# The last three gathered rows fetched in halves, and two weight chunks rounded on GpSimd

## The chip, the cores and the metric

The kernel runs on one core of one Trainium2 chip. The metric is the device time of one execution in microseconds, the median over several runs. The program is written by hand: every engine (TensorE, ScalarE, VectorE, GpSimd, and SyncE for transfers) has its own list of instructions, and semaphores tie them together.

## What is computed

Two transformer blocks follow each other on 256 tokens of width 1024. The change lies at the seam between them, so this is the part that must be seen:

```python
def block(args):                      # end of the first block: a mixture of 16384 experts
    hb, eb, gb = args
    ub = jnp.take(u, eb, axis=0)      # 8 heads x 16 experts chosen for every token
    z = jnp.einsum('thkd,td->thk', ub, hb)
    a = (jax.nn.gelu(z.astype(jnp.float32)) * gb).astype(hb.dtype)
    return jnp.einsum('thk,thkd->td', a, jnp.take(v, eb, axis=0))
...
x = x + g2[:, None, :] * rms_norm(y, norm2_post[l])      # y is the experts' sum
...
h = rms_norm_2(x, norm1_g[l])                            # the second block begins
proj = h @ w_in                                          # q, k, v, xl, gl
```

## The kernel before, in words

**Experts.** The 256 tokens are two blocks of 128 (a = 0, 1), one token to a partition. An expert's u and v rows lie side by side in one table of 2048 columns, `peer_uv`. A "row" i (0 to 255) below is one gather: for 128 tokens the i-th expert's u and v, 128 x 2048 in f32, 1 MB, 8 KB to a partition. GpSimd issues the 256 gathers in order (L2325), each as soon as its place is free (`ROW_BEFORE`: the place's row before has been combined) and its indices are there. For each row VectorE forms the dot product of the u half with the token (`dot`, L1976), ScalarE the gelu (L1318 for four rows, `last_gelu` L1332 for each of the last eight), VectorE the weight (L1987, L1994), ScalarE a diagonal matrix of it (`diagonal`, L1326), and TensorE adds diagonal times v half to two PSUM banks (L834, two matmuls, which the trace shows as four instructions). `landed(i)` is the semaphore of row i's gather; only `dot` waits for it, since everything else comes behind the dot. The last 32 rows all belong to block a = 1.

**The seam.** After row 255 ScalarE loads the table with the square root (`load_sqrt`, L1058), squares the two banks (`experts_square`, L1071), and VectorE applies the gain, the norm and the residual (`experts_norm`, L1544, L1548), and then the gain of the second block's first norm (L1544 again). TensorE transposes the two halves of the result (`feature_half`, L467), ScalarE rounds each to `hfh` (`features_hi`, L1076) and VectorE makes the rest `hfl` (`features_lo`, L1557). TensorE bridges the time with 34 products that nobody reads (L862). Block a = 0 went through the same seam long before.

**Products.** Each f32 product is made of three in a rounded format: data are split in a high part (ScalarE rounds the weights, `hi`, L1046) and a low part (VectorE subtracts, `lo`, L1514). The weights come in loads of 1 MB, each of two chunks of 128 x 1024. `WQ0 + 16` and `WQ0 + 17` are the first two chunks of q of the second block ("q2"). `token_product("q2", ...)` runs `part` for four chunks: `highs(0)` and `highs(1)` for the token blocks 0 and 1 (L501, L502), then `lows(0)`, `lows(1)` (L507). `highs(1)` of a chunk needs the features of block a = 1, `highs(0)` does not.

**Loads.** SyncE issues the weight loads (L2386). Those of the second block (I_Q2 and after) go to places that rows used: it waits for `landed(254)` and then for the combination of the last row of each place (the fifth one's is row 254). GpSimd, after its gathers, clears `wbd` once the block's features are done (L2333).

Of the kernel before, what the change touches and what calls it, by code (L numbers as in the profile page):

```python
# [10 lines left out]
AF = mybir.ActivationFunctionType  # L11
# [119 lines left out]
def build_program(nc, A, out):  # L131
# [3 lines left out]
    def sem(name):  # L135
        return ctx.enter_context(nc.semaphore(name))
# [6 lines left out]
    chunk_at = {}  # L143
    for n, (name, i, c, kind) in enumerate(chunks):
# [30 lines left out]

    s_adc = sem("s_last_adc")
    s_maxo, s_maxb = sem("s_max_out"), sem("s_max_bcast")
    s_pool, s_flp, s_id, s_const, s_wbd, s_iu = [sem("s_" + n) for n in (
        "pool", "mix_lo", "ident", "consts", "wbd0", "iu")]

# [52 lines left out]
    def landed(i):  # L233
        return s_gath[ROW_SLOT[i]], 16 * ROW_SLOT[:i + 1].count(ROW_SLOT[i])
# [175 lines left out]
    def wo_done(c):  # L410

        return s_chunk, WO0 + WO_B.index(c) + 1

    def split(n):

        assert n < WQ0 or n >= WQ0 + 16
        return n + 1 if n < WQ0 else n - 15
# [38 lines left out]
    def tensor_program(e):  # L456
# [11 lines left out]
            r.then_inc(*o.inc(s_tr, TR[mark]))  # L468

        def split_done(n):  # L470
            e.wait_ge(s_hi, split(n))
            e.wait_ge(s_lov, split(n))
            return chunk_of(n)[2:]

        def high_done(n):
            e.wait_ge(s_hi, split(n))
            return chunk_of(n)[2:]

        def product(name, f, b, xh, xl_, by_k=None):
# [10 lines left out]
                r = e.matmul(pb[:, 0:256], lo[:, k, :], xh[:, k, :], start=False, stop=k == 7)  # L490
            r.then_inc(*o.inc(s_chunk, n + 1))

        def part(n, k0, two, xh, xl_, start, stop, by_k=None, first=None, between=None):
            hi, lo = high_done(n)

            def highs(a):
                for k in range(k0, k0 + 2):
                    if by_k:
                        by_k(k, a)
                    s_ = slice(128 * a, 128 * a + 128)  # L500
                    e.matmul(two[a][:, :], xh[:, k, s_], hi[:, k - k0, :], start=start and k == k0, stop=False)  # L501
                    e.matmul(two[a][:, :], xl_[:, k, s_], hi[:, k - k0, :], start=False, stop=False)  # L502

            def lows(a):
                e.wait_ge(s_lov, split(n))
                for k in range(k0, k0 + 2):
                    r = e.matmul(two[a][:, :], xh[:, k, 128 * a:128 * a + 128], lo[:, k - k0, :], start=False,  # L507
                                 stop=stop and k > k0)
                return r

            highs(0)
            if first:
                lows(0).then_inc(*o.inc(s_first, first))
                if between:
                    between()
                highs(1)
            else:
                highs(1)
                lows(0)
            lows(1).then_inc(*o.inc(s_chunk, n + 1))  # L520

        def token_product(name, b0, b1, xh, xl_, by_k=None, first=None):
            two = [bank(b0), bank(b1)]
            for i in range(4):
                part(chunk_at[name, i], 2 * i, two, xh, xl_, i == 0, i == 3, by_k, first if i == 3 else None)
# [303 lines left out]
        for n, (a, h) in enumerate(ITS):  # L829
            for k in range(16):  # L830
                i = 16 * n + k
                e.wait_ge(s_dg, i + 1)
                for j in range(2):
                    r = e.matmul(acc[a][j][:, :], dg[:, i % 4, :], expert_rows(i)[:, 1024 + 512 * j:1536 + 512 * j],  # L834
                                 start=h == 0 and k == 0, stop=h == 7 and k == 15)
                    if i == 255 and j == 0:
                        r.then_inc(*o.inc(s_first, FIRST["y2", 0]))
                r.then_inc(*o.inc(s_comb, i + 1))
                if i == 0:
                    pb = bank(2)  # L840
                    e.wait_ge(s_q, Q_DONE[0, 1])
                    half_scores(0, 1, pb, 0).then_inc(*o.inc(s_score, SC_DONE[0, 1]))
                    frees[2] = ((s_sct, SC_DONE[0, 1]),)
                for g in QUERY_AT.get(i, ()):
                    query(g)
                if i in SCORE_AT:
                    scores(SCORE_AT[i])
                if i == 235:
                    block_features(0, (0, 1))
# [8 lines left out]

        h3_ready(7, 0)
        pb = bank(0)  # L860
        for _ in range(34):
            e.matmul(pb[:, 0:256], hfh[:, 0, 0:128], hfh[:, 0:2, 0:128], start=True, stop=True)  # L862
        for g in range(2):
            pb = bank(2 + g)
            e.wait_ge(s_hu, 6 + g + 1)
            feature_half(h2t[:, 1, :], pb, g, "h3", 2 + g)
            frees[2 + g] = ((s_flv, FLV["h3", 2 + g]),)
        token_product("q2", 0, 1, hfh, hfl, h3_ready)
        frees[0], frees[1] = ((s_qkt, 1),), ((s_qkt, 2),)
        pb = bank(4)  # L870
        e.wait_ge(s_rd, 4)
# [156 lines left out]
    def scalar_program(e):  # L1028
        o = Own(s_act)

        def hi(n):
            i, v, h, _ = chunk_of(n)
            e.wait_ge(*arrived(i))
            if n == WO0 + 1:
                e.wait_ge(s_flp, FLP["ym", 7])
            elif n == WO0 + 4:
                e.wait_ge(s_mix, 8)
                e.wait_ge(s_fhi, FHI["mix", 7])
                e.wait_ge(s_flp, FLP["mix", 7])
            elif WO0 + 3 <= n < WQ0:  # L1040
                e.wait_ge(s_chunk, WO0)
            elif WQ0 + 16 <= n < WQ0 + 19:
                e.wait_ge(s_chunk, WQ0 + 16)
            elif n >= NB and not WO0 <= n < WQ0:
                e.wait_ge(s_chunk, n - NB + 1)
            e.activation(h, v, AF.Copy).then_inc(*o.inc(s_hi, split(n)))  # L1046

        def taken(name, f):

# [338 lines left out]
            diagonal(i)  # L1388
        load_sqrt()
        experts_square(1)  # L1390
        hi(WQ0 + 16)
        block_square(1)
        hi(WQ0 + 17)
        for g in range(2):
            features_hi(1, g, banks[2 + g], "h3")
        hi(WQ0 + 18)
# [111 lines left out]
    def vector_program(e):  # L1508
        o = Own(s_vec)

        def lo(n):
            _, v, h, l = chunk_of(n)
            e.wait_ge(s_hi, split(n))
            e.tensor_tensor(l, v, h.bitcast(f32), ALU.subtract).then_inc(*o.inc(s_lov, split(n)))  # L1514

        def taken(name, f):
# [454 lines left out]
        def dot(i):  # L1971
            n, row = i // 16, expert_rows(i)[:, 0:1024]
            if i % 16 == 0:
                e.wait_ge(s_wgt, 4 * n - 4) if n >= 2 else e.wait_ge(s_h2s, 2 * n + 2)
            e.wait_ge(*landed(i))
            e.tensor_tensor_reduce(row, row, h2t[:, ITS[n][0], :], 1.0, 0.0, ALU.mult, ALU.add,  # L1976
                                   za[:, n % 2, i % 16:i % 16 + 1]).then_inc(*o.inc(s_dot, i + 1))

# [279 lines left out]
    def gpsimd_program(e):  # L2258
# [46 lines left out]
            e.dma_start(nb[:, :], A[nm][0].partition_broadcast(128)).then_inc(s_nb, 16)  # L2305


        for i in range(256):
            n = i // 16
            e.wait_ge(s_ei8, 1) if i < 8 else e.wait_ge(s_ei, n + 1)  # L2310
            if ROW_BEFORE[i] is not None:
                e.wait_ge(s_comb, ROW_BEFORE[i] + 1)
            elif ROW_SLOT[i] in SLOT_HEAD:
                e.wait_ge(s_chunk, WQ0 + 2 * SLOT_HEAD[ROW_SLOT[i]] + 2)
            elif ROW_SLOT[i] in (4, 5):
                e.wait_ge(s_lov, split(WO0 + (5, 7)[ROW_SLOT[i] - 4]))
            elif ROW_SLOT[i] == 6:
                e.wait_ge(s_tr, TR["sk", 3])
            elif ROW_SLOT[i] == 14:
                e.wait_ge(*wo_done(7))  # L2320
            else:
                e.wait_ge(s_chunk, WQ0)
            a, h = ITS[n]
            at = 16 * h + i % 16
            e.indirect_dma_start(  # L2325
                out=expert_rows(i), out_offset=None, in_=A["peer_uv"],
                in_offset=bass.IndirectOffsetOnAxis(ap=ei[:, a, at:at + 1], axis=0)).then_inc(s_gath[ROW_SLOT[i]], 16)


        e.wait_ge(s_comb, 256)  # L2330
# [11 lines left out]
    def sync_program(e):  # L2342
# [23 lines left out]
        for i in range(8, len(loads)):  # L2366
            if i == I_Q2:
                e.wait_ge(*wo_done(4))
                e.dma_start(g3[:, :], A["norm1_g_2"][0].partition_broadcast(128)).then_inc(s_n2, 16)
            if i == I_Q2 + 5:  # L2370
                e.wait_ge(s_sct, SC_DONE[6, 1])
                e.dma_start(bcs[:, 1, :], A["norm2_g_2"][0].partition_broadcast(128)).then_inc(s_n2, 16)
            if BEFORE[i] is not None:
                released(BEFORE[i])
            elif I_WQ + 6 <= i < I_Q2:
                e.wait_ge(*wo_done(i - I_WQ - 1))
            else:

                e.wait_ge(s_mix, 8)
                e.wait_ge(s_adab, 8)  # L2380
            if I_Q2 <= i < I_Q2 + 5:

                e.wait_ge(*landed(254))
                place = (12, 13, 4, 5, 6)[i - I_Q2]
                e.wait_ge(s_comb, max(r for r in range(256) if ROW_SLOT[r] == place) + 1)
            e.dma_start(places[SLOT[i]], A["weights"][i]).then_inc(s_ring[SLOT[i]], 16)  # L2386
# [34 lines left out]
```

## Time and profile before

| | |
|---|---|
| median of 3 runs | 1277.23 us (1276.95 to 1277.82) |
| the profiled execution | 1276.76 us, its span 1275.0 us |
| TensorE matmuls busy | 1144.0 us (90%) |
| VectorE / ScalarE busy | 909.6 us (71%) / 497.9 us (39%) |
| GpSimd busy | 337.0 us (26%) |
| granted TensorE clock, mean | 0.969 |
| HBM read | 404.66 MB, 318 GB/s over the span |
| chain of work that ended last | PE 43%, DMA 30%, DVE 14%, ACT 7%, issue 5% |

In the tables of the trace PE is TensorE's matmuls, PEld its weight loads, DVE VectorE, ACT ScalarE, POOL GpSimd, SPq SyncE's issue of transfers. L834 is a line of the kernel. "x4" is a number of merged instructions, and the brackets give the idle time of the engine before the row and what ended it. `in_peer_uv` gathers run on the DMA queue q0 (software), weight loads on q1 (hardware); both use the same 16 DMA engines. The experts' part runs from about 326 to 971 us.

### The profile page before, as it was taken

The page shows a single profiled execution, that of the slowest core. Times are in us where ns is not written, and L with a number is a line of the kernel's source. Part 1 is how long each engine was busy: PE and PEld are TensorE (multiplying, and loading weights), DVE is VectorE, ACT ScalarE, POOL GpSimd, SP SyncE. Part 2 cuts the span into 40 slices and gives each one's busy share as a digit, 9 for nine tenths or more (in the row PEclk, how much of TensorE's full clock was granted, in tenths as well). Part 3 has the DMA queues.
Part 4 walks back from the last instruction along what each step waited for, and adds up shares of the span by engine and source line. Part 5 has one row for each costly group of instructions (what it writes and reads, how often), then busy time and mean ns, then how long its engine had stood idle before and what let it go on. Part 6 is the DMA issues. An engine that isn't in the chain of part 4 may idle for free.

```text
span 1275.0 us, 15358 instructions
## 1 busy us (share of the span) xinstructions
PE 1144.0 (90%) x5436; PEld 811.5 (64%) x5436; DVE 909.6 (71%) x1849; ACT 497.9 (39%) x962; POOL 337.0 (26%) x311
## 2 busy tenths in 40 slices
PE   5998999999799999987788878777889999999998
PEld 4978999999655554443333433323336887999787
DVE  5985887786779767777677766677756786666544
ACT  3656454445523222222222222221524477555432
POOL 4000000000356544555554445454451000000000
PEclk8999999999899999999999988899999999999999
DMA  9874387677899999999999999999997523355550
GB/s 357 324 300 163 134 314 266 230 314 296 337 420 419 427 426 426 425 427 427 426 426 427 426 427 427 426 427 425 428 422 303 181 99 130 136 181 184 198 198 33
DMA packets 58272, 406.72 MB, mean 319 GB/s; under 512 B 6964, under 2 KB 7172, under 8 KB 9684
## 3 DMA queue, kind: packets, MB, share of 16 engines
q0 software_dynamic: 38752, 273.55, 51.3%
q1 hardware_dynamic: 19444, 132.19, 27.7%
q8 instruction: 44, 0.72, 0.2%
q14 instruction: 32, 0.26, 0.1%
HBM read 404.66 MB, written 1.06 MB: 318 GB/s over the span
## 4 chain that ended last, share of the span: by engine, by line
PE 43%; DMA 30%; DVE 14%; ACT 7%; issue 5%; POOL 1%; SPq 0%; DVEq 0%; POOLq 0%; ACTq 0%
DMA gbuf<-in_peer_uv,ei 19%; PE bank L834 11%; DMA ring<-in_peer_uv,ei 9%; PE bank L486 5%; PE bank L490 5%; PE bank L487 5%; DVE half L1514 4%; ACT half L1046 4%; PE bank L766 3%; PE bank L1020 2%; PE bank L1021 2%; PE bank L1022 2%; DMA ya<-in_weights 1%; DVE gbuf L1976 1%; PE bank L507 1%
## 5 line engine op out<-in xcount | busy, mean ns | idle before, releaser
L834 PE MATMUL bank<-gbuf,dg 128*128 128x512 f32 x540 | 260.0, 626 | 51.9 <-ACT dg L1326 51.8
L1514 DVE TENSOR_TENSOR half<-ring,half 128x1024 fp32r<-128x1024 f32 x175 | 212.7, 1222 | 123.8 <-ACT half L1046 123.5
L834 PEld LDWEIGHTS bank<-gbuf,dg 128*128 128x128 f32 x540 | 105.2, 199 | 194.2 <-issue 121.7
L1976 DVE CUSTOM_DVE_ANT_0 gbuf<-gbuf,h2t 128x1024 f32<-128x1024 f32 x135 | 165.4, 1226 | 80.8 <-DMA gbuf<-in_peer_uv,ei 78.6
L1046 ACT ACTIVATE half<-ring 128x1024 fp32r<-128x1024 f32 x175 | 182.9, 1052 | 102.2 <-PE bank L1022 45.6
L2325 POOL DMA_INDIRECT gbuf<-in_peer_uv,ei x135 | 166.1, 1230 | 182.7 <-PE bank L834 118.1
L834 PE MATMUL bank<-ring,dg 128*128 128x512 f32 x356 | 173.9, 626 | 31.6 <-ACT dg L1326 30.5
L1318 ACT ACTIVATE za<-za 128x4 f32<-128x4 f32 x62 | 12.7, 205 | 398.4 <-DVE za L1976 398.3
L2325 POOL DMA_INDIRECT ring<-in_peer_uv,ei x89 | 108.1, 1214 | 174.0 <-DVE ei L1949 76.4
L834 PEld LDWEIGHTS bank<-ring,dg 128*128 128x128 f32 x356 | 70.3, 201 | 123.6 <-issue 83.2
L1976 DVE CUSTOM_DVE_ANT_0 ring<-ring,h2t 128x1024 f32<-128x1024 f32 x89 | 108.8, 1225 | 55.6 <-DMA ring<-in_peer_uv,ei 55.1
L486 PE MATMUL bank<-hh,half 128*128 128x256 f32 x448 | 112.8, 289 | 0.9 <-DVE hl L1672 0.7
L487 PE MATMUL bank<-hl,half 128*128 128x256 f32 x448 | 110.2, 283 | 0.0
L1326 ACT ACTIVATE dg<-ident,za 128x128 f32<-128x128 f32 x256 | 82.9, 391 | 37.7 <-DVE za L1987 31.5
L486 PEld LDWEIGHTS bank<-hh,half 128*128 128x128 f32 x448 | 86.1, 192 | 1.9 <-ACT hh L1098 0.8
L487 PEld LDWEIGHTS bank<-hl,half 128*128 128x128 f32 x448 | 86.2, 192 | 0.5 <-issue 0.5
L486 PE MATMUL bank<-hfh,half 128*128 128x256 f32 x304 | 76.5, 290 | 0.0
L487 PE MATMUL bank<-hfl,half 128*128 128x256 f32 x304 | 74.4, 283 | 0.0
L490 PE MATMUL bank<-hh,half 128*128 128x256 f32 x448 | 62.8, 283 | 0.0
L486 PEld LDWEIGHTS bank<-hfh,half 128*128 128x128 f32 x304 | 58.0, 191 | 1.1
L487 PEld LDWEIGHTS bank<-hfl,half 128*128 128x128 f32 x304 | 58.1, 191 | 0.1
L490 PEld LDWEIGHTS bank<-hh,half 128*128 128x128 f32 x448 | 57.8, 192 | 0.0
(434 smaller groups left out, 1916.4 us busy)
## 6 DMA issues: line engine op xcount, KB each, us to landing
ring<-in_weights SPq DMA_DIRECT2D x114, 1024.0 KB, 5.0
gbuf<-in_weights SPq DMA_DIRECT2D x4, 1024.0 KB, 11.2
gbuf<-in_peer_uv,ei POOLq DMA_INDIRECT x135, 22.5
wq_place<-in_weights SPq DMA_DIRECT2D x2, 1024.0 KB, 6.9
bcs<-in_b_ada POOLq DMA_DIRECT2D x3, 512.0 KB, 10.9
ring<-in_peer_uv,ei POOLq DMA_INDIRECT x89
xs<-in_x SPq DMA_DIRECT2D x2, 512.0 KB, 4.3
ya<-in_weights SPq DMA_DIRECT2D x1, 1024.0 KB, 17.0
```

Source lines behind the costliest of these rows:

```text
L486: e.matmul(pb[:, 0:256], hi[:, k, :], xh[:, k, :], start=k == 0, stop=False)
L487: e.matmul(pb[:, 0:256], hi[:, k, :], xl_[:, k, :], start=False, stop=False)
L490: r = e.matmul(pb[:, 0:256], lo[:, k, :], xh[:, k, :], start=False, stop=k == 7)
L766: r = e.matmul(pb[:, s_], v[:, k, :], hf[:, k, s_], start=k == 0, stop=k == 7)
L834: r = e.matmul(acc[a][j][:, :], dg[:, i % 4, :], expert_rows(i)[:, 1024 + 512 * j:1536 + 512 * j], start=h == 0 and k == 0, stop=h == 7 an ...
L1020: e.matmul(q, l_h, hi[:, 0, s_], start=g == 0, stop=False)
L1021: e.matmul(q, l_h, lo[:, 0, s_], start=False, stop=False)
L1046: e.activation(h, v, AF.Copy).then_inc(*o.inc(s_hi, split(n)))
L1326: e.activation(dg[:, i % 4, :], ident[:, :], AF.Copy, scale=za[:, i // 16 % 2, 16 + i % 16:17 + i % 16]).then_inc(*o.inc(s_dg, i + 1))
L1514: e.tensor_tensor(l, v, h.bitcast(f32), ALU.subtract).then_inc(*o.inc(s_lov, split(n)))
L1976: e.tensor_tensor_reduce(row, row, h2t[:, ITS[n][0], :], 1.0, 0.0, ALU.mult, ALU.add, za[:, n % 2, i % 16:i % 16 + 1]).then_inc(*o.inc(s_d ...
L2325: e.indirect_dma_start(out=expert_rows(i), out_offset=None, in_=A["peer_uv"], in_offset=bass.IndirectOffsetOnAxis(ap=ei[:, a, at:at + 1], ...
```

## The change

The last three rows (253, 254, 255) are gathered as six transfers of 128 x 1024: the three u halves, then the three v halves. `dot` waits for its u half (new semaphores `s_last_u`), and TensorE waits for the v half ahead of the combination. SyncE's loads of the second block wait for the u half of row 255 instead of the whole row 254. GpSimd then rounds chunks WQ0 + 16 and WQ0 + 17 (`tensor_copy`, with a semaphore `s_q2hi` of their own), which ScalarE no longer does. TensorE runs 18 instead of 34 products that nobody reads, then `highs(0)` of both chunks (`part_highs`), and only then the two transposes.

```diff
+    def highs_of(n):
+        return (s_q2hi, n - WQ0 - 15) if WQ0 + 16 <= n < WQ0 + 18 else (s_hi, split(n) if n < WQ0 else split(n) - 2)
...
                 e.wait_ge(s_dg, i + 1)
+                if i >= 253:
+                    e.wait_ge(*landed(i))
...
         h3_ready(7, 0)
         pb = bank(0)
-        for _ in range(34):
+        for _ in range(18):
             e.matmul(pb[:, 0:256], hfh[:, 0, 0:128], hfh[:, 0:2, 0:128], start=True, stop=True)
+        two = [pb, bank(1)]
+        for i in range(2):
+            part_highs(chunk_at["q2", i], 2 * i, two, 0, hfh, hfl, i == 0)
         for g in range(2):
...
-        token_product("q2", 0, 1, hfh, hfl, h3_ready)
+        for i in range(4):
+            part(chunk_at["q2", i], 2 * i, two, hfh, hfl, i == 0, i == 3, h3_ready, done=i < 2)
...
         experts_square(1)
-        hi(WQ0 + 16)
         block_square(1)
-        hi(WQ0 + 17)
...
-            e.wait_ge(*landed(i))
+            e.wait_ge(*landed(i)) if i < 253 else e.wait_ge(s_last_u[i - 253], 16)
...
-        for i in range(256):
+        for i in range(253):
...
+        for part in range(2):
+            for i in range(253, 256):
+                a, h = ITS[15]
+                at = 16 * h + i % 16
+                if part == 0:
+                    e.wait_ge(s_comb, ROW_BEFORE[i] + 1)
+                e.indirect_dma_start(
+                    out=expert_rows(i)[:, 1024 * part:1024 * part + 1024], out_offset=None, in_=A["peer_uv"],
+                    in_offset=bass.IndirectOffsetOnAxis(ap=ei[:, a, at:at + 1], axis=0),
+                    element_offset=1024 * part).then_inc(s_gath[ROW_SLOT[i]] if part else s_last_u[i - 253], 16)
+        for c in range(2):
+            i, v, h, _ = chunk_of(WQ0 + 16 + c)
+            e.wait_ge(*arrived(i))
+            e.wait_ge(s_chunk, WQ0 + 16)
+            e.wait_ge(s_comb, 224)
+            e.tensor_copy(h, v).then_inc(*o.inc(s_q2hi, c + 1))
...
-                e.wait_ge(*landed(254))
+                e.wait_ge(s_last_u[2], 16)
```

TensorE at the seam, before (dg is the diagonal, gbuf and ring the rows' places, half_4 and half_0 the rounded chunks of q2, hfh the rounded features):

```order
L834 MATMUL bank<-gbuf,dg 128x512 [waits s_dg]
L834 MATMUL bank<-gbuf,dg 128x512
L834 MATMUL bank<-ring,dg 128x512 [waits s_dg]
L834 MATMUL bank<-ring,dg 128x512
L834 MATMUL bank<-gbuf,dg 128x512 [waits s_dg]
L834 MATMUL bank<-gbuf,dg 128x512
L862 MATMUL bank<-hfh 128x256 [waits s_feat_lo,s_feat_hi]
L862 MATMUL bank<-hfh 128x256 x33
L467 MATMUL bank<-ident,h2t 128x128 [waits s_h_gained,s_q]
```

and now:

```order
L847 MATMUL bank<-gbuf,dg 128x512 [waits s_gather3,s_dg]
L847 MATMUL bank<-gbuf,dg 128x512
L847 MATMUL bank<-ring,dg 128x512 [waits s_gather6,s_dg]
L847 MATMUL bank<-ring,dg 128x512
L847 MATMUL bank<-gbuf,dg 128x512 [waits s_gather7,s_dg]
L847 MATMUL bank<-gbuf,dg 128x512
L875 MATMUL bank<-hfh 128x256 [waits s_feat_lo,s_feat_hi]
L875 MATMUL bank<-hfh 128x256 x17
L505 MATMUL bank<-half_4,hfh 128x512 [waits s_q2_high,s_feat_lo]
...
L505 MATMUL bank<-half_0,hfh 128x512 [waits s_q2_high]
...
L473 MATMUL bank<-ident,h2t 128x128 [waits s_h_gained,s_q]
```

The last three rows have a wait for their gather, and eight products of q2 stand ahead of the transposes in place of 16 unread ones.

GpSimd and SyncE at the end of the gathers, now (before, GpSimd had three gathers of 128x2048 in place of the six and went from them to `wbd`, and SyncE's five loads waited for s_gather6, row 254):

```order
L2349 DMA gbuf<-in_peer_uv,ei 128x1024 [waits s_combine]
L2349 DMA ring<-in_peer_uv,ei 128x1024 [waits s_combine]
L2349 DMA gbuf<-in_peer_uv,ei 128x1024 [waits s_combine]
L2349 DMA gbuf<-in_peer_uv,ei 128x1024
L2349 DMA ring<-in_peer_uv,ei 128x1024
L2349 DMA gbuf<-in_peer_uv,ei 128x1024
L2358 CAST half_4<-ring 128x1024 [waits s_combine,s_chunk,s_ring4]
L2358 CAST half_0<-ring 128x1024 [waits s_combine,s_chunk,s_ring4]
L2364 MEMSET wbd 128x1024 [waits s_feat_hi,s_feat_lo,s_combine]
...
L2417 DMA ring<-in_weights 128x2048 [waits s_combine,s_last_u2] x2
```

The gathers' order is u 253, 254, 255, then v 253, 254, 255, and the two roundings stand behind them.

## Rows read from the trace of the kernel before

**Rows 1.** VectorE, order of time, dots of rows 252 to 255: start, length, what, idle before

```profile
960.04 1.23 DVE L1976 CUSTOM_DVE_ANT_0 gbuf<-gbuf,h2t 128x1024 f32<-128x1024 f32 x1 [0.72 <-DMA gbuf<-in_peer_uv,ei]
...
962.48 1.22 DVE L1976 CUSTOM_DVE_ANT_0 gbuf<-gbuf,h2t 128x1024 f32<-128x1024 f32 x1 [0.71 <-DMA gbuf<-in_peer_uv,ei]
...
964.98 1.23 DVE L1976 CUSTOM_DVE_ANT_0 ring<-ring,h2t 128x1024 f32<-128x1024 f32 x1 [0.77 <-DMA ring<-in_peer_uv,ei]
...
967.40 1.23 DVE L1976 CUSTOM_DVE_ANT_0 gbuf<-gbuf,h2t 128x1024 f32<-128x1024 f32 x1 [0.70 <-DMA gbuf<-in_peer_uv,ei]
```

**Rows 2.** TensorE, order of time, 955 to 989 us

```profile
955.26 12.18 PE L834 MATMUL bank<-gbuf,dg 128*128 128x512 f32 x28
967.27 1.90 PE L834 MATMUL bank<-ring,dg 128*128 128x512 f32 x4
969.61 1.98 PE L834 MATMUL bank<-gbuf,dg 128*128 128x512 f32 x4 [0.44 <-ACT dg L1326]
971.03 4.62 PE L862 MATMUL bank<-hfh 128*128 128x256 f32 x34
975.75 1.29 PE L467 MATMUL bank<-ident,h2t 128*128 128x128 f32 x8
...
977.35 0.39 PE L501 MATMUL bank<-half,hfh 128*128 128x512 f32 x1
977.58 0.40 PE L502 MATMUL bank<-half,hfl 128*128 128x512 f32 x1
978.37 0.47 PE L501 MATMUL bank<-half,hfh 128*128 128x512 f32 x1 [0.40 <-DVE hfl L1557]
```

**Rows 3.** ScalarE, order of time, after the last diagonal

```profile
969.64 1.28 ACT L1058 ACT_TABLE_LOAD   x1
...
971.04 0.58 ACT L1071 ACTIVATE pk<-bank 128x512 f32<-128x512 f32 x1
...
971.63 0.60 ACT L1071 ACTIVATE pk<-bank 128x512 f32<-128x512 f32 x1
...
975.91 1.04 ACT L1046 ACTIVATE half<-ring 128x1024 fp32r<-128x1024 f32 x1
976.85 1.06 ACT L1076 ACTIVATE hfh<-bank 128x512 fp32r<-128x512 f32 x2
```

**Rows 4.** VectorE, order of time, the norms and the features

```profile
971.74 0.69 DVE L1544 TENSOR_TENSOR h2t<-bank,bcs 128x512 f32<-128x512 f32 x1 [2.62 <-ACT pk L1071]
...
977.53 0.69 DVE L1557 TENSOR_TENSOR hfl<-bank,hfh 128x512 fp32r<-128x512 f32 x1 [0.99 <-ACT hfh L1076]
...
980.07 3.49 DVE L1514 TENSOR_TENSOR half<-ring,half 128x1024 fp32r<-128x1024 f32 x3
```

**Rows 5.** DMA packets by queue (number, MB, share of 16 engines), 962.2 to 965 us

```profile
q0 software_dynamic: 10, 0.07, 6.2%
```

**Rows 6.** The same, 965.5 to 966 and 966.5 to 967 us

```profile
q1 hardware_dynamic: 7, 0.06, 95.2%
q0 software_dynamic: 2, 0.02, 7.7%
...
q1 hardware_dynamic: 12, 0.10, 53.6%
q0 software_dynamic: 1, 0.01, 3.9%
```

**Rows 7.** The same, 45.5 to 46 us, loads beside a broadcast of 4 KB rows

```profile
q1 hardware_dynamic: 15, 0.12, 58.7%
q0 software_dynamic: 16, 0.07, 32.8%
```

**Rows 8.** SyncE's issues at the seam (five loads)

```profile
964.97 4.62 SPq L2386 DMA_DIRECT2D ring<-in_weights  x5
```

**Rows 9.** GpSimd, order of time: gathers of rows 253 to 255, and `wbd`

```profile
946.47 0.94 POOL L2325 DMA_INDIRECT gbuf<-in_peer_uv,ei  x1 [0.30 <-issue]
948.18 1.64 POOL L2325 DMA_INDIRECT ring<-in_peer_uv,ei  x1 [0.77 <-PE bank L834]
952.76 1.96 POOL L2325 DMA_INDIRECT gbuf<-in_peer_uv,ei  x1 [2.94 <-PE bank L834]
980.07 0.98 POOL L2333 MEMSET wbd<- 128x1024 f32 x1 [25.35 <-DVE hfl L1557]
```

**Rows 10.** Stretches: us, busy of PE, PEld, DVE, ACT, POOL; then granted clock, DMA, GB/s

```profile
887.54:890.95 3.41, 0.47 (x2) 0.00 (x0) 2.88 (x9) 0.20 (x1) 1.99 (x2) 1.00 1.02 432
890.95:894.36 3.41, 2.96 (x4) 1.40 (x5) 2.41 (x5) 3.36 (x8) 0.00 (x0) 0.50 1.01 428
945.56:948.98 3.42, 1.85 (x5) 0.54 (x3) 2.22 (x4) 0.00 (x0) 2.34 (x3) 1.00 1.01 402
```

More of the change, by code:

```diff
@@ L177, in build_program @@
     s_maxo, s_maxb = sem("s_max_out"), sem("s_max_bcast")
+    s_last_u = [sem(f"s_last_u{i}") for i in range(3)]
+    s_q2hi = sem("s_q2_high")
     s_pool, s_flp, s_id, s_const, s_wbd, s_iu = [sem("s_" + n) for n in (
@@ L470, in split_done @@
         def split_done(n):
-            e.wait_ge(s_hi, split(n))
+            e.wait_ge(*highs_of(n))
             e.wait_ge(s_lov, split(n))
@@ L475, in high_done @@
         def high_done(n):
-            e.wait_ge(s_hi, split(n))
+            e.wait_ge(*highs_of(n))
             return chunk_of(n)[2:]
@@ L491, in product, with part_highs, part @@
             r.then_inc(*o.inc(s_chunk, n + 1))
-        def part(n, k0, two, xh, xl_, start, stop, by_k=None, first=None, between=None):
+        def part_highs(n, k0, two, a, xh, xl_, start, by_k=None):
+            hi = high_done(n)[0]
+            for k in range(k0, k0 + 2):
+                if by_k:
+                    by_k(k, a)
+                s_ = slice(128 * a, 128 * a + 128)
+                e.matmul(two[a][:, :], xh[:, k, s_], hi[:, k - k0, :], start=start and k == k0, stop=False)
+                e.matmul(two[a][:, :], xl_[:, k, s_], hi[:, k - k0, :], start=False, stop=False)
+        def part(n, k0, two, xh, xl_, start, stop, by_k=None, first=None, between=None, done=False):
             hi, lo = high_done(n)
             def highs(a):
[L497 to L502, printed above, removed]
+                part_highs(n, k0, two, a, xh, xl_, start, by_k)
             def lows(a):
@@ L509, in lows @@
                 return r
-            highs(0)
+            if not done:
+                highs(0)
             if first:
@@ L1045, in hi @@
                 e.wait_ge(s_chunk, n - NB + 1)
-            e.activation(h, v, AF.Copy).then_inc(*o.inc(s_hi, split(n)))
+            e.activation(h, v, AF.Copy).then_inc(*o.inc(*highs_of(n)))
         def taken(name, f):
@@ L1512, in lo @@
             _, v, h, l = chunk_of(n)
-            e.wait_ge(s_hi, split(n))
+            e.wait_ge(*highs_of(n))
             e.tensor_tensor(l, v, h.bitcast(f32), ALU.subtract).then_inc(*o.inc(s_lov, split(n)))
```

## The prediction

> **What bounds the kernel now.** I read the chain of waits first: over the experts' part it alternates between gathers and dots, so that part runs at the rate of the gathers. Then I read the engines in order of time around the seam. The dots of rows 252 to 255 start at 960.04, 962.48, 964.98 and 967.40, each after waiting for its row [rows 1]: 2.44 us to a row. TensorE is hardly behind: rows 247 to 253 are one unbroken run of 28 instructions over 12.0 us, 1.72 us to a row, then row 254 at 967.27 and row 255 at 969.61, after a wait for the diagonal [rows 2]. From that start, call it C, everything up to the features is a chain across three engines, and from 978.37 on TensorE runs products without a gap. So the end moves with C, with the time from C to VectorE's `hfl` of the first half (977.53, call it X [rows 4]), and with what TensorE still has to do after X. I take all later stages to move one for one.
>
> One more thing is to be seen before the sum. From 962.2 to 965 us there are only ten packets (nine of 8 KB, by the 0.07 MB, and a tiny one), 6.2% of 16 engines [rows 5], that is 0.31 us each, one after the other without a gap: **a single DMA engine** lags, the other 15 are through with the gathers, and a row has landed when that one has.
>
> **The change part by part.**
>
> *Halves.* If the lagging engine moves the same bytes at the same rate, the u halves land 1.22 us apart behind row 252: row 253's dot could start at 961.3, and the u half of 255 is in at about 963.8. The three dots then follow VectorE's own pace. Dot, gelu and weight took some 1.75 us together (the weight's end comes 0.7 us before the next dot of [rows 1]), so the last dot starts near 965.3, not 967.40. The last diagonal is ready by 967.5. The v half of 255 lands where the row did, 967.4. Then TensorE sets C: row 253 at 965.1 as before (12.0 us for seven rows), 254 at 966.85, 255 at **968.57**, 1.04 earlier. A packet of 4 KB took 32.8% of 8.0 us over 16, 0.164 us, against 0.309 for 8 KB [rows 5, 7]: at most 0.02 x 24 = 0.45 us more over the six halves, at least nothing. I take 0.2: last u half 963.9, last v half 967.6.
>
> *GpSimd's issues.* Three more gathers at 0.94 to 1.96 us each [rows 9] stand behind the u half of row 255 (952.76), so the v halves go out by about 960, and the first is due at 963.9. Hidden, with some 4 us to spare.
>
> *SyncE's loads.* This is where I chose. They waited for row 254 (964.97 [rows 8]) and now go at 963.9, while three v halves are still outstanding on the lagging engine. How do the two queues share an engine? At 45.5 us, with 8 KB load packets beside 4 KB packets of the other queue, there were 15 of one and 16 of the other in half a microsecond [rows 7]: they take turns, packet by packet, so a half gets 0.16 us out of every 0.47. When does the load reach the lagging engine? In the kernel before, the load was issued at 964.97, seven load packets had started on other engines by 966 [rows 6], and row 255 was still not slowed: 2.42 us behind row 254 [rows 1], its last 8 KB packet beginning between 966.5 and 967 [rows 6]. So the load came to this engine 1.8 us or more after its issue, where others had it after 1.0. With 963.9 + 1.8 = 965.7 and the v halves' bytes ending at 967.25 (0.35 before the 967.6 at which the dependent engine would start), 1.55 us or ten packets of 4 KB remain, and each has a load packet of 0.31 us before it: 3.1 us more. The last v half is then seen at 970.7, and **C is 970.7, 1.1 us later than before**. Both ends: nothing (C = 968.57) and the full stretch from 1.0 us on (964.9, 15 packets, 4.65 us, C = 972.3).
>
> By the Trainium skill ("DMA: Bandwidth & Descriptors", Queues, rings and completion order) an engine drains a whole packet of typically 9 to 17 descriptors from one queue before it switches. By that the last half would wait for about one row's share of a load, 8 x 0.31 = 2.5 us, and C would be 970.1.
>
> *From C to X.* Before, X came 7.92 us after C. Now the table load of 1.28 us [rows 3] runs while TensorE waits, so the squares no longer start 1.43 and 2.02 after C but some 0.3 and 0.1 sooner. TensorE: the row 1.72, 18 unread products at 4.62/34 = 0.136 make 2.45, and eight products of q2 at 0.23 (977.35 to 977.58 [rows 2]) make 1.82; the transposes start at C + 6.0, 0.14 sooner. ScalarE began the first half's features at 976.85, when it came out of the second rounding (975.91 [rows 3]); without that it starts when the first four transposes are done, C + 6.65. **X is C + 7.3, a gain of 0.6.** The first rounding stood in ScalarE's idle time; taking it away gives nothing.
>
> *GpSimd's rounding* of 128 x 1024: not in the trace. The nearest rows are its memset of the same size, 0.98 [rows 9], and ScalarE's rounding, 1.04 [rows 3]; I take 1.1 and as the bad end three times that. The first load has landed near 970.2 (it shares the lagging engine, total bytes unchanged), so the copies end at 971.3 and 972.4. TensorE asks for them at C + 4.2 and C + 5.1, 974.9 and 975.8. Hidden; even at 2.7 us each they are nearly in time.
>
> *After X.* The four products of the second chunk's `highs(0)` are done already: 4 x 0.23 = **0.9 less**. The first chunk's four stood in a gap anyway. VectorE's low parts now become nearly late: the first of three from 980.07 [rows 4] ends 3.7 us behind X, and TensorE asks for it at X + 3.7. I count nothing.
>
> The sum: +1.1 - 0.6 - 0.9 = **-0.4 us**. It is made against the profiled execution (1276.76 us; the median is 1277.23, 0.5 above) and carried over to the median: **1276.8 us**. A measurement of this kernel can tell about 0.2%, 2.55 us, from no change.
>
> **The rivals.**
>
> *The loads do not disturb the halves* (the lagging engine gets its share still later, or takes the older queue first). Row 255's undisturbed 2.42 us speaks for it, the turns in [rows 7] against. Then C = 968.57: -1.04 - 0.6 - 0.9 = -2.5 us, 1274.7. Chance 0.22; about half of it lies beyond 0.2%.
>
> *Slower: the load arrives early and TensorE stands still too long.* With C = 972.3 the sum is +2.7 - 1.5 = +1.2. TensorE would be idle for 3.7 us from 968.6. A stretch in which it was busy for 0.47 of 3.41 us was followed by 3.41 us at 0.50, that is 1.2 GHz, while 1.85 busy left it at 1.00 [rows 10]. Half clock over the row, the unread products and part of q2 costs up to 1.7 us: +2.9, 1280.1. [...] Chance 0.08.
>
> *It does not do what it says.* The rounding on GpSimd is three times dearer, and TensorE's queue stands before the transposes: the second copy ends at 970.2 + 6.6 = 976.8, 1.0 us behind TensorE's demand, +0.6 in all, 1277.8. Or a half's packets cost nearly those of a row. Chance 0.07.
>
> My forecast has the remaining 0.63.
>
> **How the numbers follow.** The range goes from the first rival with its own uncertainty, 1274.5, to a middle of the slower cases, 1278.9. Faster by over 0.2%: half of the first rival, 0.11. Slower by over 0.2%: 0.07. Within: 0.82.
>
> **What would show it.** In the changed kernel's trace: dots of 253 to 255 about 1.75 us apart, the last near 965.3; SyncE's first load near 963.9; TensorE's row 254 near 967 and row 255 only at 970.7, with 2 us of idleness ended by a DMA; q0 packets beyond 967 beside q1 packets; `hfl` 7.3 us behind row 255; the end of q2's last chunk 10.2 us behind `hfl`, where it was 11.1. If row 255 starts at 968.6 my reading of the queues is wrong; if TensorE waits for GpSimd, the rounding's price is; and if q2 ends earlier but the whole does not, a later stage has its own limit.

## The result, and the profile after

The changed kernel takes **1275.11 us** (median of 20 runs, 1274.09 to 1276.75), the kernel before in the same comparison 1277.19 us (20 runs, 1276.40 to 1278.42). The ratio is 0.9985, 95% interval 0.9978 to 0.9991: 2.1 us less, 0.15%. That lies within the 0.2% that I called no change, and inside the range. But 20 runs resolve it, and it is five times the forecast of -0.4 us: it lies nearest to the first rival's sum of -2.5.

The profiled execution took 1276.75 us, at the slow end of the runs of this kernel; its span is 1275.0 us, as before, and the mean granted clock 0.969. That the spans are equal says nothing of the seam, as the last two table rows below show. I name four points: **T**, the start of row 252's dot; **C**, the start of row 255's combination; **X**, the start of `hfl`; and **E**, the end of q2 (the weight load of the product behind it, 0.23 us ahead of the matmul's own row).

| us | before | after | forecast of the difference | measured |
|---|---|---|---|---|
| T to C | 9.57 | 9.00 | +1.1 | -0.57 |
| C to X | 7.92 | 7.21 | -0.6 | -0.71 |
| X to E | 10.86 | 10.08 | -0.9 | -0.78 |
| T to E, sum | 28.35 | 26.29 | -0.4 | **-2.06** |
| T itself | 960.04 | 961.23 | 0 | +1.19 |
| E to VectorE's last group | 281.29 | 282.16 | 0 | +0.87 |

T itself differs from execution to execution: it lies between 959.05 and 961.23 in every profile of this document but "loads behind 248", the kernel before's among them. So all is measured from T.

VectorE in order of time, which answers to [rows 1, 4] (start, length, what, idle before):

```profile
961.23 1.23 DVE L1991 CUSTOM_DVE_ANT_0 gbuf<-gbuf,h2t 128x1024 f32<-128x1024 f32 x1 [0.74 <-DMA gbuf<-in_peer_uv,ei]
...
962.87 1.22 DVE L1991 CUSTOM_DVE_ANT_0 gbuf<-gbuf,h2t 128x1024 f32<-128x1024 f32 x1
...
964.51 1.22 DVE L1991 CUSTOM_DVE_ANT_0 ring<-ring,h2t 128x1024 f32<-128x1024 f32 x1
...
966.14 1.22 DVE L1991 CUSTOM_DVE_ANT_0 gbuf<-gbuf,h2t 128x1024 f32<-128x1024 f32 x1
...
973.72 1.42 DVE L1563 SCALAR_TENSOR_TENSOR xs<-h2t,sm,xs 128x512 f32<-128x512 f32 x2
...
977.44 0.69 DVE L1572 TENSOR_TENSOR hfl<-bank,hfh 128x512 fp32r<-128x512 f32 x1 [0.58 <-ACT hfh L1093]
```

The last three dots wait for no transfer any more and follow each other after 1.64 us, where it was 2.44. TensorE in order of time, to [rows 2]:

```profile
956.50 12.18 PE L847 MATMUL bank<-gbuf,dg 128*128 128x512 f32 x28
968.51 1.88 PE L847 MATMUL bank<-ring,dg 128*128 128x512 f32 x4
970.23 1.88 PE L847 MATMUL bank<-gbuf,dg 128*128 128x512 f32 x4
971.55 2.71 PE L875 MATMUL bank<-hfh 128*128 128x256 f32 x18
974.10 0.40 PE L505 MATMUL bank<-half,hfh 128*128 128x512 f32 x1
...
976.08 1.29 PE L473 MATMUL bank<-ident,h2t 128*128 128x128 f32 x8
978.28 0.47 PE L505 MATMUL bank<-half,hfh 128*128 128x512 f32 x1 [0.91 <-DVE hfl L1572]
```

There is no bracket on row 255 at 970.23: TensorE goes through its queue at 1.72 us to a row and never waits for a v half. The wait that my sum was built on is not there. The one before the first product that needs `hfl` grew from 0.40 [rows 2] to 0.91: TensorE now comes there earlier.

ScalarE, to [rows 3]; GpSimd's roundings and SyncE's loads, to [rows 9, 8]:

```profile
968.37 1.28 ACT L1075 ACT_TABLE_LOAD   x1
...
971.35 0.60 ACT L1088 ACTIVATE pk<-bank 128x512 f32<-128x512 f32 x1 [1.48 <-PE bank L847]
```

```profile
971.22 2.02 POOL L2358 CAST half<-ring 128x1024 fp32r<-128x1024 f32 x2 [12.84 <-DMA ring<-in_weights]
```

```profile
964.97 5.84 SPq L2417 DMA_DIRECT2D ring<-in_weights  x5
```

The table load ran while TensorE combined row 254, and the squares waited for TensorE alone. A rounding of 128 x 1024 on GpSimd takes 1.03 us (both 2.02 with their overlap); I had taken 1.1. Both are over by 973.2, and TensorE asks for the first at 974.1.

The loads were issued 3.74 us behind T, as I had assumed (1.2 us earlier than before against T). DMA packets by queue (number, MB, share of 16 engines), 964 to 965, 967 to 968, and 968.4 to 968.9 us, to [rows 5, 6]:

```profile
q0 software_dynamic: 7, 0.02, 6.0%
...
q1 hardware_dynamic: 47, 0.39, 91.1%
q0 software_dynamic: 7, 0.02, 6.0%
...
q1 hardware_dynamic: 25, 0.20, 96.6%
```

Before any load moves and with the loads in full flow on the other engines, it is the same 7 packets in a microsecond: 6.0% of 16 us is 0.96 us, one engine, with no room for a load's packet between them. The lagging engine moved the halves as if no load had been issued. Its last 4 KB packet ends at 968.36, 3.39 us behind SyncE's first issue, and from 968.4 on the loads fill all 16 engines.

Two stretches far behind the seam, in the columns of [rows 10], of after and then the same two of before:

```profile
1085.90:1089.30 3.40, 1.59 (x13) 1.41 (x14) 2.91 (x5) 0.90 (x2) 0.00 (x0) 1.00 0.79 275
1089.31:1092.72 3.41, 3.41 (x19) 3.41 (x18) 1.62 (x2) 2.45 (x6) 0.00 (x0) 0.50 0.09 34
```

```profile
1085.90:1089.30 3.40, 1.58 (x13) 1.20 (x12) 3.22 (x6) 0.60 (x1) 0.00 (x0) 1.00 0.47 149
1089.31:1092.72 3.41, 3.33 (x27) 3.15 (x28) 1.30 (x3) 2.77 (x6) 0.00 (x0) 1.00 0.38 156
```

In this one execution after fell to 0.50 (1.2 GHz) behind a stretch of 1.59 us of work, before stayed at 1.00 behind 1.58; the instructions through the stretch are 19 instead of 27. The profiled executions fall in two groups here: 281.2 to 281.4 us from E to the end without this fall, and 282.2 with it. It costs 0.9 us and is not the change's: a second profile of the changed kernel (below) has 281.26, and the kernel before with one number altered has 282.17.

### The profile page after: what moved, and what is told of

Same layout as the page of the kernel before. It is cut to its first block, busy times and chain, and to the rows that moved or that the text cites. A ratio compares the mean times of both kernels' runs of the same rounds, so it can differ in the third digit from the quotient of the medians.

```text
span 1275.0 us, 15352 instructions
## 1 busy us (share of the span) xinstructions
PE 1140.1 (89%) x5420; PEld 809.1 (63%) x5420; DVE 909.9 (71%) x1849; ACT 496.3 (39%) x960; POOL 333.2 (26%) x316
## 4 chain that ended last, share of the span: by engine, by line
PE 46%; DMA 30%; DVE 12%; ACT 6%; issue 4%; POOL 1%; SPq 0%; POOLq 0%; DVEq 0%
DMA gbuf<-in_peer_uv,ei 15%; DMA ring<-in_peer_uv,ei 13%; PE bank L847 12%; PE bank L492 5%; PE bank L496 5%; PE bank L493 5%; DVE half L1529 4%; ACT half L1063 3%; PE bank L777 2%; PE bank L1037 2%; PE bank L1039 2%; PE bank L1038 2%; PE bank L517 2%; DMA row_place<-in_peer_uv,ei 1%; PE bank L505 1%
## 5 line engine op out<-in xcount | busy, mean ns | idle before, releaser
L847 PE MATMUL bank<-gbuf,dg 128*128 128x512 f32 x540 | 256.6, 619 | 50.6 <-ACT dg L1343 50.5
L2340 POOL DMA_INDIRECT gbuf<-in_peer_uv,ei x133 | 158.7, 1193 | 180.1 <-PE bank L847 119.6
L2340 POOL DMA_INDIRECT ring<-in_peer_uv,ei x88 | 104.7, 1190 | 175.6 <-DVE ei L1964 76.8
```

Source lines behind the costliest of these rows:

```text
L2340: e.indirect_dma_start(out=expert_rows(i), out_offset=None, in_=A["peer_uv"], in_offset=bass.IndirectOffsetOnAxis(ap=ei[:, a, at:at + 1], ...
```

## The experiments

My theory after the result: the halves bring their undisturbed gain, because the loads reach the lagging engine later than I put it; the seam's two terms stand. The rivals: the older queue is served first, so turns never happen here; or the gain is the seam's alone.

All times below are read as in the table above, each from one profiled execution. "Casts" are GpSimd's roundings. Where the interval of the ratio holds 1.0000 (halves only, loads late, loads behind u 254, before from 244, ScalarE rounds), the medians alone do not tell the run from the kernel before, and what is said of it rests on its trace.

| run | T to C | C to X | X to E | T to E | E to end | median, and before beside it | ratio, 95% |
|---|---|---|---|---|---|---|---|
| halves only | 8.95 | 7.63 | 10.86 | 27.44 | 281.28 | 1276.25 / 1277.29 | 0.9992 (0.9983 to 1.0002) |
| rounding only | 10.65 | 7.21 | 10.11 | 27.96 | 281.29 | 1276.01 / 1277.29 | 0.9989 (0.9980 to 0.9998) |
| loads late | 10.36 | 7.52 | 10.10 | 27.97 | 282.26 | 1276.72 / 1277.29 | 0.9998 (0.9989 to 1.0007) |
| loads behind 248 | 13.71 | 7.22 | 10.05 | 30.97 | 281.34 | 1286.38 / 1277.29 | 1.0076 (1.0060 to 1.0091) |
| loads behind 252 | 16.25 | 7.29 | 10.06 | 33.60 | 281.24 | 1282.07 / 1276.79 | 1.0042 (1.0026 to 1.0057) |
| loads behind u 254 | 10.10 | 7.29 | 10.03 | 27.43 | 281.26 | 1276.23 / 1276.79 | 0.9993 (0.9984 to 1.0003) |
| singles from 244 | 8.55 | 7.21 | 10.07 | 25.84 | 282.18 | 1275.60 / 1276.97 | 0.9988 (0.9979 to 0.9997) |
| singles from 240 | 8.55 | 7.21 | 10.07 | 25.82 | 281.28 | 1275.12 / 1276.97 | 0.9985 (0.9976 to 0.9994) |
| before, from 244 | 9.55 | 7.92 | 10.85 | 28.32 | 282.17 | 1277.77 / 1276.97 | 1.0006 (0.9997 to 1.0015) |
| ScalarE rounds | 9.00 | 9.47 | 10.09 | 28.56 | 281.34 | 1277.90 / 1276.97 | 1.0009 (1.0000 to 1.0018) |
| two rows halved | 8.19 | 7.28 | 10.06 | 25.52 | 281.24 | 1274.97 / 1276.79 | 0.9985 (0.9976 to 0.9994) |
| changed again | 8.95 | 7.21 | 10.06 | 26.22 | 281.26 | 1274.55 / 1276.79 | 0.9985 (0.9976 to 0.9994) |

### Halves only

TensorE's 34 unread products and ScalarE's roundings are back (GpSimd's are gone).

```diff
-        for _ in range(18):
+        for _ in range(34):
...
-            part_highs(chunk_at["q2", i], 2 * i, two, 0, hfh, hfl, i == 0)
...
+        hi(WQ0 + 16)
         block_square(1)
+        hi(WQ0 + 17)
```

> The kernel before with the halves alone (and the loads of the second block waiting for the last u half); ScalarE rounds both chunks and TensorE's order is the old one. Measured from T, the start of row 252's dot. Theory 'three separate gains' (the row 255 starts when TensorE has worked off its queue; the load does not disturb): row 255's combination starts at T + 9.0 as in the changed kernel (T + 9.6 before), the first low part of the features 7.7 behind it (7.9 before), the last q2 product unchanged 11.1 behind that: 0.8 us faster than before. Rival 'the seam's order does it all': the early start is eaten by ScalarE's second rounding, and the end moves by less than 0.3.

T to E is 0.91 shorter than before, the median 1.04 (the interval of its ratio just holds 1). TensorE in order of time:

```profile
966.85 1.88 PE L847 MATMUL bank<-ring,dg 128*128 128x512 f32 x4
968.57 1.88 PE L847 MATMUL bank<-gbuf,dg 128*128 128x512 f32 x4
974.42 1.29 PE L473 MATMUL bank<-ident,h2t 128*128 128x128 f32 x8
```

No wait for a half here either. C gains 0.62, and another 0.29 comes between C and X, since the table load no longer stands behind C. X to E is unchanged to 0.01: that term belongs to the seam alone.

### Rounding only

Whole rows again (256 gathers, `dot` and SyncE wait for whole rows, TensorE for none); the rest as changed.

```diff
-                e.wait_ge(s_last_u[2], 16)
+                e.wait_ge(*landed(254))
```

> The changed kernel with whole rows again: rows 253 to 255 as three gathers of 128x2048, loads waiting for row 254, GpSimd's rounding and TensorE's new order kept. Theory 'three separate gains': row 255 starts at T + 9.6 (before's value), the features' low part 7.4 to 7.5 behind it, q2's last product 10.2 behind that: 1.3 us faster than before. Rival 'the gain is in the halves': within 0.5 us of before. GpSimd's copies: 1.0 us each, done before TensorE asks.

The median is 1.28 less. In its profile C is late, 10.65, and this is not the edit's doing: a stretch at half clock fell on TensorE's combinations.

```profile
947.00:950.40 3.40, 0.81 (x3) 0.40 (x3) 1.86 (x4) 1.29 (x5) 1.83 (x2) 1.00 1.00 424
950.50:953.90 3.40, 3.40 (x5) 1.35 (x4) 2.18 (x5) 0.88 (x4) 0.29 (x1) 0.50 1.01 429
```

With before's 9.57 in its place T to E would be 26.89, 1.46 less than before. That is a little too kind, since a late C hides some of the table load as well. The two halves of the change together (0.91 + 1.46) thus exceed the whole (2.06) by 0.3: both claim the same 0.3 between C and X.

### The loads moved: late, and three steps early

One line of SyncE in each, against the changed kernel:

```diff
-                e.wait_ge(s_last_u[2], 16)
+                e.wait_ge(*landed(255))
```

That is "loads late". The three others have `*landed(248)`, `*landed(252)` and `s_last_u[1], 16` there.

> The changed kernel, with SyncE's loads of the second block held until the whole of row 255 has landed (3.5 us later). If the loads disturb the v halves, row 255's combination starts earlier than T + 9.0. If they do not (theory of the changed kernel's trace: the lagging engine serves its gathers first), T + 9.0 stays, but the first load lands about 3 us later, GpSimd's copies end near T + 15 and TensorE waits for them before the transposes: the features 1 to 2.5 us later, so 1 to 2.5 us slower than the changed kernel.

> The changed kernel, with SyncE's loads waiting for row 248 only: two of them can then go 15 us earlier, in the full stream of gathers, the next two when rows 245 and 246 are combined. Theory 'the two queues take turns on every engine, packet by packet': rows 249 to 255 are slowed, their dots 4 to 5 us apart instead of 2.44 while loads are outstanding, row 255's combination up to 9.8 us later (4 MB at 2.44 us each), 5 to 9 us slower than the changed kernel. Theory 'an engine finishes the gathers it has before it takes a load': dots stay 2.44 apart, row 255 at T + 9.0, same time or slightly faster.

> The changed kernel, with SyncE's loads waiting for row 252 instead of the last u half: 3.7 us earlier, at T. In the run with loads at row 248 the first load packets ran 3.55 us after the issue, on every engine, and then took turns with the gathers. Theory 'a busy engine takes a load 3.5 us after its issue, then turns': packets of loads reach the lagging engine at T + 3.6, when 3.6 us of 4 KB packets (23) are left, each then behind a load packet of 0.31: the last v half 7 us later, row 255's combination at T + 14 to 15 instead of 9.0, some 5 us slower than the changed kernel. Theory 'the lagging engine serves gathers first': T + 9.0.

> The changed kernel, with SyncE's loads waiting for the u half of row 254, 1.25 us earlier, at T + 2.5. By the same theory the loads reach the lagging engine at T + 6.0, when about 1.1 us or 7 packets are left: the last v half lands 2.2 us later, row 255's combination at T + 9.7 to 10 instead of 9.0, 0.7 to 1 us slower than the changed kernel. Rival: no difference.

**Do the queues take turns?** Yes. With the loads issued 16 us ahead of T, the dots, which were 2.44 us apart, come 4.93 and 4.97 apart (VectorE in order of time):

```profile
956.88 1.23 DVE L1991 CUSTOM_DVE_ANT_0 gbuf<-gbuf,h2t 128x1024 f32<-128x1024 f32 x1 [2.01 <-DMA gbuf<-in_peer_uv,ei]
...
961.85 1.22 DVE L1991 CUSTOM_DVE_ANT_0 gbuf<-gbuf,h2t 128x1024 f32<-128x1024 f32 x1 [3.25 <-DMA gbuf<-in_peer_uv,ei]
```

and its packets from 955.2 to 957.2 us are

```profile
q1 hardware_dynamic: 68, 0.56, 68.4%
q0 software_dynamic: 68, 0.27, 33.1%
```

68 and 68, one for one, the same as in [rows 7]. The rival "the older queue first" is dead as a standing rule.

**From when?** The same run says that too. The loads were issued at 950.68 (SyncE, then the packets by queue from 953.5 to 954.2 and from 954.2 to 955 us):

```profile
950.68 5.66 SPq L2417 DMA_DIRECT2D ring<-in_weights  x4
```

```profile
q0 software_dynamic: 66, 0.26, 101.8%
...
q1 hardware_dynamic: 26, 0.21, 69.4%
q0 software_dynamic: 30, 0.11, 35.5%
```

No load packet runs on any of the 16 engines until 954.2, **3.55 us** after the issue, though here all were busy with gathers. In the changed kernel 15 engines are idle, and between 966 and 966.3 us, 1.0 to 1.3 after the issue at 964.97, there were already

```profile
q1 hardware_dynamic: 6, 0.05, 111.0%
```

With the loads behind u 254 (issue 962.75, 2.51 us behind T) the two cases stand side by side. In the trace the lagging engine's 4 KB packets begin every 0.155 us up to 966.13, and then at 966.60, 967.06, 967.52, every 0.46. The packets by queue, 964.2 to 966.2 and 966.2 to 968.2 us:

```profile
q1 hardware_dynamic: 83, 0.68, 83.3%
q0 software_dynamic: 15, 0.05, 6.5%
...
q1 hardware_dynamic: 117, 0.84, 99.5%
q0 software_dynamic: 4, 0.02, 2.0%
```

The first load packet on the engine still busy with gathers is the one between 966.13 and 966.60: it begins at 966.29, 3.54 us after the issue, while the idle engines have been moving the load since 963.74. Row 255 then waits (TensorE):

```profile
970.34 1.96 PE L847 MATMUL bank<-gbuf,dg 128*128 128x512 f32 x4 [0.99 <-DMA gbuf<-in_peer_uv,ei]
```

Behind 252 (issue 960.31, first load packet on that engine at 963.87, 3.56 us later) TensorE waits for all three v halves, rows 253, 254 and 255:

```profile
968.12 1.96 PE L847 MATMUL bank<-gbuf,dg 128*128 128x512 f32 x4 [2.15 <-DMA gbuf<-in_peer_uv,ei]
972.84 1.96 PE L847 MATMUL bank<-ring,dg 128*128 128x512 f32 x4 [2.77 <-DMA ring<-in_peer_uv,ei]
976.56 1.96 PE L847 MATMUL bank<-gbuf,dg 128*128 128x512 f32 x4 [1.76 <-DMA gbuf<-in_peer_uv,ei]
```

C comes 7.25 us late; I had expected some 5. Three issues, and on an engine with gathers outstanding the turns begin 3.54, 3.55 and 3.56 us behind each (behind 248 that is the first of 16 engines). By that they would begin at 968.5 in the changed kernel, and the lagging engine's last half was done at 968.36: missed by less than 0.2 us. Issued 1.25 us earlier the load costs 1.2 us, 3.7 us earlier 7.3. I see no room to loosen SyncE's wait any further.

**Is the load under way for so long?** No. Where the lagging engine has no gathers left, its share of the load starts sooner. In the kernel before its last gather ends at 967.06, and in the run with two rows halved (issue 965.60) at 967.67, both 2.1 us behind the issue. From then on the loads fill all 16 engines: 15 of them would make 93.75% (packets of the kernel before, 967.1 to 969.3 us, then of two rows halved, 967.7 to 969.5):

```profile
q1 hardware_dynamic: 121, 0.90, 98.8%
...
q1 hardware_dynamic: 91, 0.75, 98.4%
```

So the load can run on that engine 2.1 us after its issue, and with gathers outstanding the engine still serves them alone until 3.5 us. By these rows, what was late in the changed kernel is the beginning of the turns, and not the load.

**Does standing still lower the clock?** Not always. That was the slower rival's second half. Behind 252 TensorE waits for 6.7 us in all and the granted clock stays at 1.00 through the seam; behind 248 it falls to 0.50 (1.2 GHz) from 968.2 to 978.4 us. One stretch of each, in the columns of [rows 10]:

```profile
973.60:977.00 3.40, 1.64 (x4) 0.49 (x3) 0.00 (x0) 0.00 (x0) 0.00 (x0) 1.00 0.40 107
...
968.20:971.60 3.40, 2.61 (x3) 1.18 (x4) 1.32 (x2) 0.45 (x2) 0.00 (x0) 0.50 0.81 335
```

By the ratios "loads behind 248" is 11.6 us slower than the changed kernel, where I had expected 5 to 9; this fall is part of it.

By the Trainium skill ("DMA: Bandwidth & Descriptors", Queues, rings and completion order) an engine switches queues only after a whole packet of typically 9 to 17 descriptors. Once the turns have begun, the runs show a switch after every single row of 4 or 8 KB; the measurement decides.

**Late.** With the loads behind row 255's landing the median is 1.6 us above the changed kernel's. Its profile again has C late behind a half-clock stretch, so it can't show whether C would have come earlier than T + 9.00, and it shows no wait of TensorE for the casts. An estimate: with C at T + 9.00 TensorE would ask for the first at C + 3.87, that is 973.6, and this cast ends at 974.1, so the casts would cost some 0.5 us. The rest of the 1.6 us stays open. The profile does show something else (GpSimd, then VectorE):

```profile
973.07 2.03 POOL L2358 CAST half<-ring 128x1024 fp32r<-128x1024 f32 x2 [13.92 <-DMA ring<-in_weights]
```

```profile
974.59 1.72 DVE L1563 SCALAR_TENSOR_TENSOR xs<-h2t,sm,xs 128x512 f32<-128x512 f32 x2
```

VectorE's residual, which reads two tensors, takes 1.72 us for the two beside GpSimd's copy, and 1.42 in the changed kernel, where the copy is over. Hence 7.52 from C to X instead of 7.21. The Trainium skill ("GPSIMD Engine Reference", Specifications) says that GpSimd shares SBUF interfaces with VectorE, with contention when VectorE's instruction has two SBUF inputs; this agrees.

### Can C move further?

C gained 0.57 and not 1.04, as TensorE was some 0.4 us further behind than I had it: it goes from row 244 to row 255 without a pause. `LAST` is the row from which gelu, weight and diagonal go row by row rather than in fours. Smaller, TensorE should catch up.

```diff
-    LAST = 248
+    LAST = 244
```

The next has 240 there, and the third is the kernel before with 244.

> The changed kernel with the weights of rows 244 to 247 made row by row (LAST = 244), so that TensorE starts on row 244 some 7 us earlier and has no queue at row 253. Theory 'TensorE's queue of whole rows sets the start of row 255 in the changed kernel': the start moves from T + 9.0 to the landing of the last v half or the last diagonal, T + 7.3 to 7.6, and the time falls by 1.4 us more. Rival 'the last gathers set it': T + 9.0 stays and the time is the same.

> As LAST = 244, for rows 240 to 247. No queue is left to remove: T + 7.3 to 7.6 again, the time that of LAST = 244 within 0.5 us. If single weights slow the dots, the rows fall behind their landing and it is slower.

> The kernel before with LAST = 244 alone. There row 255 waited for its landing, dot and diagonal, not for TensorE's queue: start at T + 9.6, unchanged, and the same time as before within 0.4 us. If this is faster by 1 us or more, the queue mattered before too.

The run with 240 leaves out one operation, the reciprocal of the last head's softmax sum. Both gain 0.45 on C, where I had expected 1.4 to 1.7, and the medians show nothing of it (ratios 0.9988 and 0.9985, the changed kernel 0.9985). The next wait is seen at once (TensorE, singles from 244):

```profile
965.11 1.96 PE L847 MATMUL bank<-gbuf,dg 128*128 128x512 f32 x4 [0.85 <-DMA gbuf<-in_peer_uv,ei]
966.90 1.88 PE L847 MATMUL bank<-ring,dg 128*128 128x512 f32 x4
968.62 1.88 PE L847 MATMUL bank<-gbuf,dg 128*128 128x512 f32 x4
```

TensorE has caught up and now stands for the v half of **253**, which the order u, u, u, v, v, v makes the fourth half behind row 252, where the whole row was the first two: at 1.22 us a half, 2.4 us later. Two more rows at 1.72 follow. I had not seen that the first v half, not the last, would bind. In the kernel before, with whole rows, the same edit moves nothing (9.55).

### Two rows halved

Rows 254 and 255 alone in halves, with singles from 244.

```diff
-                if i >= 253:
+                if i >= 254:
...
-        for i in range(253):
+        for i in range(254):
...
-            for i in range(253, 256):
+            for i in range(254, 256):
```

> The changed kernel with LAST = 244 and only rows 254 and 255 in halves. With LAST = 244 and three halved rows TensorE waited for the v half of row 253 (T + 5.0) and the two rows after it cost 1.72 each, so row 255 started at T + 8.55. Here row 253 lands whole at T + 2.4 and is done by T + 6; the v half of 254 lands at about T + 6.2, so row 255 starts at T + 7.9: 0.6 us faster than with three, 1.1 faster than the changed kernel, about 3.1 faster than before. Rival 'the last v half is later than that' (T + 7.5): start no better than T + 8.3.

C comes at 8.19, the shortest of all, though I had expected 7.9; T to E is 0.7 less than in the changed kernel (TensorE, row 253, which has no transfer to wait for):

```profile
965.34 1.98 PE L847 MATMUL bank<-gbuf,dg 128*128 128x512 f32 x4 [0.46 <-ACT dg L1343]
```

In the medians that can't be told: 1274.97 beside 1274.55 for the changed kernel again. I can't name a version that beats the changed one.

### ScalarE rounds, TensorE in the new order

```diff
+        hi(WQ0 + 16)
         block_square(1)
+        hi(WQ0 + 17)
...
-            e.tensor_copy(h, v).then_inc(*o.inc(s_q2hi, c + 1))
```

> The changed kernel with both chunks rounded on ScalarE at their old places, TensorE's new order kept. TensorE then stands before the second chunk's products until ScalarE has done its second rounding, 7.1 us behind the start of row 255, and the transposes come behind them: transposes at +8.1 instead of +5.9, the features' low part at +9.5 instead of +7.2, 2 us slower than the changed kernel. Rival 'which engine rounds does not matter': within 0.5 us.

The transposes come at C + 8.13 instead of 5.85 and X at C + 9.47. ScalarE's second rounding stands behind the block's squares, and TensorE's queue stands before it:

```profile
975.15 0.50 PE L505 MATMUL bank<-half,hfh 128*128 128x512 f32 x1 [1.86 <-ACT half L1063]
...
976.18 1.04 PE L473 MATMUL bank<-ident,h2t 128*128 128x128 f32 x8
```

T to E is 28.56, 0.2 more than in the kernel before and 1.1 more than with the halves only: without GpSimd's rounding the new order takes back more than the halves bring. Against the changed kernel it is 2.3 us, and 3.1 by the ratios (1.0009 and 0.9985 of 1277).

### The changed kernel again

> The changed kernel once more, on the same chip as the other three, so that they can be compared: T + 9.0, the features 7.2 behind, q2's end 10.1 behind that, the time 0.9985 of before. Its time after q2's end should be 281.3 us where the clock is never granted at half speed there and 282.2 where it is once, as in the profile that was shown.

T to E is 26.22, 2.13 less than before, its span 1272.6, and the ratio the same as the first time.

## Why the prediction was right, and where it was wrong

The time fell in the range and within the 0.2% to which I gave 0.82, but by the rival to which I gave 0.22. That it came out right is in part luck and owed to the width of the range: the main path of the forecast did not happen.

- **The step that failed: "the load came to this engine 1.8 us or more after its issue".** That was a lower bound, taken from a kernel in which nothing disturbed row 255; I put it into the sum as if it were the moment from which the engine takes turns. With gathers outstanding the turns begin 3.54 to 3.56 us after the issue. With that the halves' bytes end before the first turn, 3.1 us of turns become none, and the term +1.1 becomes the -0.57 measured. It was also two things taken for one: the load can run on that engine 2.1 us after its issue, and the engine does not take turns then if it still has gathers. The rule of the turns, on which I spent most words, was right, one for one, and did not matter. What the rows of before could have told was only that the first turn was later than 966.8; the rival ("gets its share still later") deserved at least half.
- **C without disturbance was mis-sized.** I had row 253 at 965.1 and row 254 at 966.85 from "12.0 us for seven rows". But the run of seven begins at 955.26, so its last row, 253, comes near 965.6, and [rows 2] has row 254 at 967.27 with no wait before it: TensorE's queue sets it. C gained 0.57 to 0.62, not 1.04.
- **C to X**: -0.6 forecast, -0.71 measured. The transposes came at C + 5.85 for 6.0. The halves alone give 0.29 of it.
- **X to E**: -0.9 forecast, -0.78 measured, and all of it from the four products moved.
- **GpSimd**: the issues of the six halves were hidden, the roundings at 1.03 us never waited for. Costed at nothing, rightly; with the same rounding left on ScalarE the seam is 2.3 us longer.
- **The slower rival** needed turns that made TensorE stand still, and then half clock. For a load issued earlier than this kernel does, the first half is true (loads behind 252: 6.7 us of waits, ratio 1.0042). The second half did not follow there, and did in "loads behind 248".

Sum by the measured terms: -0.57 - 0.71 - 0.78 = -2.06, beside -2.08 in the medians.

Open: what keeps an engine at its gathers until 3.5 us after a load's issue, when the load could run there after 2.1; where the rest of the 1.6 us of "loads late" goes; and why 1.59 us of work in a stretch was followed by half clock and 1.58 was not.

## What to carry to other kernels

A bound that you read from a trace ("not before 1.8 us") is not a value, and the moment at which a transfer can run is not the moment at which it gets its turn: when the sum hangs on it, ask what the next larger value would do, and give that case its share of the chance. When the last rows of a stream are fetched in halves, halve as few as the compute engines need, because every u half put forward delays the first v half (T to C 8.55 us with three rows halved, 8.19 with two; the medians do not resolve it). And when an in-order engine is given new work ahead of a critical step, move that work's own inputs off the critical engines first.

## What the runs showed of the hardware that I had not expected

- A load issued by SyncE began on the first idle DMA engine 1.0 us after its issue, on the lagging engine 2.1 us after it where the gathers had just ended (the kernel before, two rows halved), and 3.54 to 3.56 us after it on engines with gathers outstanding (three issues). The Trainium skill ("DMA: Bandwidth & Descriptors", Latency and other measured facts) gives some 0.6 us to the first byte; no run here shows it that short.
- One DMA engine finishes its share of the gathers some 5 us behind the other 15: in the changed kernel a single one moves halves from 963 to 968.4 us.
- Once they take turns, the two queues share an engine one for one by rows, though the rows differ in size: beside 8 KB packets, 4 KB packets begin every 0.46 us instead of 0.155.
- A copy of 128 x 1024 on GpSimd stretches VectorE's operations with two inputs from 1.42 to 1.72 us for two.
- One stretch of 3.4 us at 0.50 in the second block costs 0.9 us, and comes in some executions and not in others (4 of the 14 profiles). TensorE's waits of 2.15, 2.77 and 1.76 us in "loads behind 252" were followed by no such stretch.
